# Attention loop unrolled with the softmax one head ahead, and a new order at the passage to the experts

## The chip, the cores and the metric

One core of one Trainium2 chip. The metric is the device time of one execution in microseconds (us), lower is better. The matrix engine (PE), the vector engine (DVE), the scalar engine (ACT), the small-step engine (POOL, GpSimd) and the queue that issues most weight transfers (SP, SyncE) each run a program of their own, and meet only at semaphores.

## What is computed

One layer over 256 prompt frames and 32 sample frames (288 rows, model width 2048), in float32:

```python
h = rms_norm(x, g_mix)
q_sb, k_sb, v_sb, q_sw, k_sw, v_sw, gate_pre = split(h @ w_in)    # 8 heads x 128; SWA has 2 kv heads
o_sb = stick_breaking(q_sb, k_sb, v_sb)        # exp(log_sigmoid(z) + sum of later log_sigmoid(-z))
o_sw = swa(rope(q_sw), rope(k_sw), v_sw, sink) # window of 2 chunks of 64, softmax with a sink
g = sigmoid(gate_pre + b_gate)
x = x + (g_sb * (o_sb @ w_sb_o) + g_swa * (o_sw @ w_swa_o)) @ w_out
x = x + hier_moe(rms_norm(x, g_ffn))           # best group of 4, then 2 of its 4 gated experts
y = rms_norm(x, g_final)
```

The sample frames attend to 128 cached frames besides their own. New keys and values are outputs as well, in float32.

## The kernel before

Float32 accuracy is reached by splitting each operand into a high and a low part and adding three products (L958, L959, L960 in `products`). A "block" is 128 output columns: 16 steps of 128 rows by three matmuls of 288 columns, 48 matmuls. For each block ACT makes the high part of the weights (`wh`, L635) and DVE the low part (`wl`, L1328, in `split`); SP fetches the weights into a ring, two blocks at a time.

The stages follow one another on PE:

- Projections: Q, K, V of the stick-breaking part, Q of the sliding window, then two K and two V blocks (KVSW). During the first, POOL zeroes the 4.5 MB of `y_rows` that overflowing experts would use: one memset and five DMAs of up to 1 MB.
- Sample attention: for each of the two kv groups, one after the other, scores (PE), maximum (DVE), exponent (ACT), divide (DVE, `zw`, L1426), transpose (PE, L1022), copy (ACT, L716), product with the values (PE, L1026).
- Attention: 8 heads in a loop over pairs. A head on PE is: scores `z`, a gate block, the suffix sums C (L1059), the transposes of the window's probabilities `zw` (L1066), a gate block, the two value products (L1073 and on). Softplus (ACT `lg`, DVE `spb`) and softmax (ACT L703, DVE L1426) of a head lie between its own `z` and its own C. ACT changes its table twice in a head (Exp to Ln and back).
- Second products: `o` of both attentions is split by ACT (`oh`, 16 copies of 288 columns) and DVE (`ol`, 16 subtractions); then 32 blocks, gates and products in turn, merged into `m` (parts `mh`, `ml`, L1478).
- Last projection: 16 blocks k. After block k PE runs, for block k-1, `turn_x` (transposes of the new residual times the norm weight, `xg`) and `logits` (router, needs `wr`, scaled by DVE in L1526). DVE adds the residual into `xT` (L1486); `xT` is fetched from HBM by a POOL DMA at the start of this stage. After each fourth block ACT and DVE cut the transposed residual into three bf16 parts (`parts_high` on ACT, `parts_rest` on DVE with `x2r`, L1495) for the exact gather.
- Passage and experts: routing on DVE, `choose` (L1613) makes the 0/1 matrix `pick` that gathers 64 slots for an expert on PE (L1157). 16 experts have 12 weight pieces of 1 MB each; a hand-written ORDER lists the 192 pieces, and at each piece t ACT makes its high part (L372), DVE its low part (L367, `slot_lo`), PE the products (L1176, L1179). `further_steps` and `row_numbers` (L1670 to L1721: slot weights, counts, the row numbers of the final gather) run on DVE at t = 2. `slot_rms` (PE) collects the norm of the slots.
- End: indirect gather of each token's two expert rows, weighted sum, final norm.

The lines at the last projection:

```python
for k in range(KT):
    pe.wait_ge(S["ev_d"], EV_OUT_D + k)
    products(IT_OUT + k // 4, k % 4, mh, ml)
    if k:
        turn_x(k - 1)
        pe.wait_ge(S["wr_scaled"], 1)
        logits(k - 1)
```

Of the kernel before, what the change touches and what calls it, by code (L numbers as in the profile page):

```python
# [173 lines left out]
def build(nc, x_prompt, x_sample, cache_sb_k, cache_sb_v, cache_swa_k, cache_swa_v, w_in, b_gate, swa_sink,  # L174
# [45 lines left out]
    st = at("st", 189.25, [P, 16])  # L220
    kcw_nat = at("kcw_nat", 189.5, [P, KV * HD])
    rope_a = at("rope_a", 181, [P, NT])
    rope_b = at("rope_b", 182.25, [P, NT])
    zero = at("zero", 184, [P, 512])
# [39 lines left out]
    stack_b = at("stack_b", 205.90625, [TAIL, DEC], BF16)  # L264
# [55 lines left out]
    with ExitStack() as ctx:  # L320
# [189 lines left out]
        def _(pool):  # L510
# [43 lines left out]
            for n in range(2):  # L554
                with pool.Fori(0, 2) as ii:
                    i = ii + 2 * n
                    for j in range(4):
# [4 lines left out]
                        else:  # L562
# [5 lines left out]
                              sb_kv_sample[ds(i, 1)].rearrange("a p n -> p (a n)"))  # L568
            pool.wait_ge(S["rope_done"], 11)

            for g in range(KV):
                pool.tensor_copy(qst[:, g * P:(g + 1) * P].rearrange("p (h n) -> p h n", h=GRP),
                                 qT[:, H + GRP * g:H + GRP * g + GRP, SEQ:NT]).then_inc(S["qst_st"], 1)
            pool.wait_ge(S["nat_done"], 21)
            pool.tensor_copy(v_sw[:], nat[:, :, KV * HD:]).then_inc(S["pool_head"], 1)
            nat_store(4, nat[:, 1, :], swa_kv_prompt, swa_kv_new)

            pool.wait_ge(S["pool_head"], 18)  # L580
            pool.wait_ge(S["vc_in"], 16)
            pool.wait_ge(S["kc_sb"], 2)
            with pool.Fori(0, IT_PROJ - IT_ATT) as i:
                for u in range(2):
                    hd = i * 2 + u
                    pool.wait_ge(S["z_sb"], hd + 1)
                    pool.tensor_copy(kst[:, 0:3, :], kT_sb[:, ds(hd, 1), :].rearrange("p a (t n) -> p (a t) n", n=P))\
                        .then_inc(S["kst_st"], 1)
                    pool.tensor_copy(kst[:, 3:4, :], kcT_sb[:, ds(hd, 1), :]).then_inc(S["kst_st"], 1)
                    pool.wait_ge(S["z_sw"], hd + KV)  # L590
                    pool.tensor_copy(qst[:].rearrange("p (a n) -> p a n", a=1),
                                     qT[:, ds(i + (H + GRP * u), 1), 0:SEQ]).then_inc(S["qst_st"], 1)
                    pool.wait_ge(S["o_sb"], hd + 1)
                    pool.tensor_copy(vst[:, 0:3, :], v_sb[:, :, ds(hd * P, P)]).then_inc(S["vst_st"], 1)
                    pool.tensor_copy(vst[:, 3:4, :], vc_sb[:, ds(hd * P, P)].rearrange("p (a n) -> p a n", a=1))\
                        .then_inc(S["vst_st"], 1)
# [22 lines left out]
        def _(act):  # L619
# [70 lines left out]
            act.wait_ge(S["pool_head"], 17)  # L690
            for j in range(4):
                step(IT_KVSW, j, None if j < 2 else lambda: a_.activation(
                    headT[:, j, 0:NT], main(j), ACT.Copy).then_inc(S["ev_a"], 1))
            act.wait_ge(S["kc_ps"], 3)
            a_.activation(kcT_sw[:], ps[6][:, 0:KV * P].rearrange("p (h n) -> p h n", h=KV), ACT.Copy)\
                .then_inc(S["kc_sb"], 1)

            def softmax(segments, sink, n):

                act.wait_ge(S["zw_done"], n)
                for c, (a, b) in enumerate(segments):
                    a_.activation(zw[:, a:b], zw[:, a:b], ACT.Exp, bias=st[:, 2 + c:3 + c],  # L703
                                  accum_out=st[:, 4 + c:5 + c]).then_inc(S["sums_done"], 1)
                c = len(segments)
                a_.activation(st[:, 6:6 + c], st[:, 2:2 + c], ACT.Exp, bias=sink).then_inc(S["sums_done"], 1)

            act.wait_ge(S["small_in"], 16 * 13)
            for g in range(KV):  # L710
                softmax([(0, SSC)], sinks_s[:, g:g + 1], g + 1)
                act.wait_ge(S["pT_ps"], g + 1)
                if g:
                    act.wait_ge(S["o_sw"], g)
                a_.activation(pT[:, 0:P], ps[5][:, 0:P], ACT.Copy).then_inc(S["pT_sb"], 1)
                a_.activation(pT[0:DEC, P:2 * P], ps[5][0:DEC, P:2 * P], ACT.Copy).then_inc(S["pT_sb"], 1)  # L716
                act.wait_ge(S["o_sw"], g + 1)
                a_.activation(qT[:, H + GRP * g:H + GRP * g + GRP, SEQ:NT],
                              ps[7][:, 0:P].rearrange("p (h n) -> p h n", h=GRP), ACT.Copy)\
                    .then_inc(S["o_sw_ev"], 1)  # L720
# [3 lines left out]
            with act.Fori(0, IT_PROJ - IT_ATT) as i:  # L724
                own.enter(i, 4)
                for u in range(2):
                    hd = i * 2 + u

                    act.wait_ge(S["zm_done"], hd + 2)
                    own(a_.activation(lg[:], zm[:], ACT.Abs))  # L730
                    own.wait()
                    own(a_.activation(lg[:], lg[:], ACT.Exp, scale=-1.0))
                    own.wait()
                    a_.activation(lg[:], lg[:], ACT.Ln, bias=1.0).then_inc(S["l_done"], 1)
                    softmax([(0, P), (P, SWC)], sinks[:, ds(i + GRP * u, 1)], hd + (KV + 1))

                    def gate(j):
                        return lambda: a_.activation(flat(gates[:, ds(i * 4 + j, 1), :]), main(j), ACT.Identity,
                                                     bias=par[:, ds(i * 4 + j, 1)]).then_inc(S["ev_a"], 1)
                    step(i + IT_ATT, 2 * u, gate(2 * u))  # L740
                    act.wait_ge(S["e_done"], hd + 2)
                    a_.activation(spb[:], lg[:], ACT.Exp).then_inc(S["a_done"], 1)
                    act.wait_ge(S["pT_ps"], hd + (KV + 1))
                    act.wait_ge(S["o_sw"], hd + KV)
# [10 lines left out]
            for h in range(2 * H):  # L755
                a_.activation(oh[:, h, :], qT[:, h, :], ACT.Copy).then_inc(S["oh_done"], 1)
# [4 lines left out]
            for r0 in (0, DEC, 2 * DEC):  # L761
                a_.activation(stack_b[r0:r0 + DEC, :], con[r0:r0 + DEC, r0:r0 + DEC], ACT.Copy)\
                    .then_inc(S["ident_done"], 1)
# [1058 lines left out]
```

## Time and profile before

| what | value |
|---|---|
| median of 3 runs | 1393.62 us (1389.62 to 1393.69) |
| profiled execution, its own time | 1389.65 us |
| its span | 1387.9 us |
| PE busy | 1237.8 us, 89% |
| DVE busy | 923.9 us, 67% |
| ACT busy | 790.1 us, 57% |
| mean granted PE clock | 0.968 of full speed |
| moved by DMA | 345.71 MB, 249 GB/s |

The span is what the profile covers; 1.7 us lie around it. A row in brackets such as [4.33 <-DVE wl L1328] says that the engine was idle for 4.33 us before this instruction, and that the end of DVE's instruction for `wl` of line 1328 let it go on. The granted clock is a share of 2.4 GHz: 1.00 is 2.4 GHz, 0.50 is 1.2 GHz.

### The profile page before, as it was taken

The numbers are of one execution on the slowest core, as the hardware profiler recorded it, in microseconds if no ns is written. First come the engines' busy times: TensorE is split into PE (matmuls) and PEld (weight loads), VectorE is DVE, ScalarE is ACT, GpSimd is POOL, SyncE is SP. The second block draws the span as 40 slices with busy tenths as digits, with TensorE's granted clock in tenths as the row PEclk, the third lists the DMA queues.
The fourth block names the chain that finished last, engine by engine and source line by source line (L and its number), as shares of the span: only waits on it lengthen the run. The fifth ranks groups of instructions, "written<-read, shape, count | busy, mean of one in ns | idle before, by whom it ended". The sixth has DMA issues, their size and how long they took to land.

```text
span 1387.9 us, 21824 instructions
## 1 busy us (share of the span) xinstructions
PE 1237.8 (89%) x8964; PEld 1079.3 (78%) x8964; DVE 923.9 (67%) x902; ACT 790.1 (57%) x761; POOL 63.9 (5%) x109
## 2 busy tenths in 40 slices
PE   5889999979999899999999957999999999999861
PEld 3789999969898899999899945666676666666650
DVE  3633345644444545454455585999999999999967
ACT  3423333235655744544444454888888888888852
POOL 2100010011221000000000000000000000000010
PEclk9999999989999999999999978999999999999995
DMA  8484545441322353553645756999999999999954
GB/s 262 154 302 152 186 146 190 169 145 61 121 96 86 123 171 130 181 181 128 243 146 187 296 199 224 363 410 413 414 414 414 416 416 414 414 413 413 416 186 171
DMA packets 187155, 345.71 MB, mean 249 GB/s; under 512 B 5328, under 2 KB 107840, under 8 KB 176080
## 3 DMA queue, kind: packets, MB, share of 16 engines
q1 hardware_dynamic: 182352, 322.72, 62.7%
q0 software_dynamic: 4336, 18.53, 3.8%
q10 hardware_dynamic: 400, 3.51, 0.6%
q8 instruction: 49, 0.80, 0.2%
q14 instruction: 18, 0.15, 0.0%
HBM read 321.86 MB, written 23.07 MB: 249 GB/s over the span
## 4 chain that ended last, share of the span: by engine, by line
PE 49%; DVE 34%; ACT 8%; issue 4%; DMA 4%; ACTq 0%; DVEq 0%; POOL 0%; POOLq 0%; SPq 0%
DVE slot_lo L367 24%; PE bank L958 14%; PE bank L960 13%; PE bank L959 13%; ACT eh L372 3%; PE bank L1176 3%; DVE y_sb L1653 2%; ACT wh L635 2%; DMA ring<-in_w_in 1%; DVE hgx L1632 1%; PE bank L1186 1%; PE bank L936 1%; DVE wl L1328 1%; DMA con<-in_const 1%; DMA yb<-y_rows,rows 1%
## 5 line engine op out<-in xcount | busy, mean ns | idle before, releaser
L367 DVE TENSOR_TENSOR slot_lo<-slot,eh 128x2048 fp32r<-128x2048 f32 x192 | 431.4, 2280 | 11.9 <-ACT eh L372 11.9
L372 ACT ACTIVATE eh<-slot 128x2048 fp32r<-128x2048 f32 x192 | 359.8, 1908 | 31.4 <-PE bank L1179 16.3
L1328 DVE TENSOR_TENSOR wl<-ring,wh 128x2048 fp32r<-128x2048 f32 x100 | 229.1, 2293 | 212.5 <-ACT wh L635 212.4
L958 PE MATMUL bank<-xh,wh 128*128 128x288 f32 x1088 | 331.6, 305 | 9.7 <-DVE xl L1336 5.1
L959 PE MATMUL bank<-xl,wh 128*128 128x288 f32 x1088 | 324.1, 298 | 0.0
L960 PE MATMUL bank<-xh,wl 128*128 128x288 f32 x1088 | 323.3, 297 | 0.0
L635 ACT ACTIVATE wh<-ring 128x2048 fp32r<-128x2048 f32 x100 | 190.8, 1909 | 131.0 <-PE bank L960 120.5
L958 PEld LDWEIGHTS bank<-xh,wh 128*128 128x128 f32 x1088 | 206.7, 190 | 14.5 <-issue 8.4
L959 PEld LDWEIGHTS bank<-xl,wh 128*128 128x128 f32 x1088 | 207.7, 191 | 0.3
L960 PEld LDWEIGHTS bank<-xh,wl 128*128 128x128 f32 x1088 | 207.9, 191 | 0.0
L1176 PE MATMUL bank<-slot_lo,hgx 128*128 128x512 f32 x512 | 146.1, 408 | 28.5 <-DVE slot_lo L367 26.6
L1176 PE MATMUL bank<-eh,hgx 128*128 128x512 f32 x512 | 150.8, 417 | 5.0 <-DVE hgx L1632 3.7
L1176 PEld LDWEIGHTS bank<-slot_lo,hgx 128*128 128x128 f32 x512 | 93.9, 191 | 67.8 <-DVE slot_lo L367 49.4
L1176 PEld LDWEIGHTS bank<-eh,hgx 128*128 128x128 f32 x512 | 90.1, 193 | 19.3 <-DVE hgx L1632 4.2
L1157 PEld LDWEIGHTS bank<-pick,x 128*128 128x128 bf16 x1536 | 60.3, 101 | 40.6 <-issue 32.7
L1179 PE MATMUL bank<-slot_lo,aTx 128*128 128x512 f32 x256 | 72.9, 406 | 10.5 <-DVE slot_lo L367 9.9
L958 PE MATMUL bank<-mh,wh 128*128 128x288 f32 x256 | 77.2, 302 | 2.7 <-DVE ml L1478 2.7
L958 PE MATMUL bank<-oh,wh 128*128 128x288 f32 x256 | 76.6, 299 | 3.3 <-DVE wl L1328 3.3
L1157 PE MATMUL bank<-pick,x 128*128 128x64 bf16 x1536 | 71.3, 197 | 7.2 <-DVE pick L1613 7.2
L959 PE MATMUL bank<-ol,wh 128*128 128x288 f32 x256 | 76.3, 298 | 0.0
L960 PE MATMUL bank<-oh,wl 128*128 128x288 f32 x256 | 75.9, 297 | 0.0
L959 PE MATMUL bank<-ml,wh 128*128 128x288 f32 x256 | 75.5, 295 | 0.0
(319 smaller groups left out, 1508.4 us busy)
## 6 DMA issues: line engine op xcount, KB each, us to landing
ring<-in_w_in SPq DMA_DIRECT2D x34, 2048.0 KB, 7.9
slot<-in_w_e_gate SPq DMA_DIRECT2D x64, 1024.0 KB, 10.2
slot<-in_w_e_up SPq DMA_DIRECT2D x64, 1024.0 KB, 9.8
slot<-in_w_e_down SPq DMA_DIRECT2D x64, 1024.0 KB, 10.7
ring<-in_w_out SPq DMA_DIRECT2D x8, 2048.0 KB, 8.0
ring<-in_w_sb_o SPq DMA_DIRECT2D x8, 1024.0 KB, 5.1
ring<-in_w_swa_o SPq DMA_DIRECT2D x8, 1024.0 KB, 7.4
y_rows<-y_sb SPq DMA_DIRECT2D x15, 512.0 KB, 10.0
```

The lines of the kernel that those rows point to most:

```text
L367: v.tensor_tensor(slot_lo[i][:], slot[i][:], eh[t % EH][:].bitcast(F32), ALU.subtract)\
L372: a_.activation(eh[t % EH][:], slot[t % CH][:], ACT.Copy).then_inc(S["hi_ready"], 1)
L635: a_.activation(wh[:, j % 2], raw(j), ACT.Copy).then_inc(S["wh_ready"], 1)
L936: mm = tr(ps[2 + k % 3][:, t * P:t * P + n], x_nat[0:n, t, k * P:(k + 1) * P], ident[0:n, 0:n])
L958: mm_(dst, wh[:, j % 2, k, :], hi[:, k, :], start=(k == k0), stop=False)
L959: mm_(dst, wh[:, j % 2, k, :], lo[:, k, :], start=False, stop=False)
L960: mm = mm_(dst, wl[:, j % 2, k, :], hi[:, k, :], start=False, stop=(k == k1 - 1))
L1157: mm_(out, x2[j][:, t, k * P:(k + 1) * P], p_[:, t, 0:SLOTS], start=(t == 0 and j == 0), stop=False)
L1176: mm = mm_(ps[2 + j // 4], hgx[:, kt, :], part[:, c * 512:(c + 1) * 512], start=(low == 0 and kt == 0), stop=(low == 1 and kt == KT - 1))
L1179: mm = mm_(ps[bank0 + c], aTx[par_][:, j - 8, :], part[:, c * 512:(c + 1) * 512], start=(low == 0 and j == 8), stop=(low == 1 and j == CH ...
L1328: v.tensor_tensor(wl[:, j % 2], raw(j), wh[:, j % 2].bitcast(F32), ALU.subtract)\
L1653: v.tensor_tensor(y, y, banks[0:SLOTS, y_banks(s, h)], ALU.add).then_inc(S["y_dve"], 1)
```

## The change

1. The zeroing of `y_rows` moves from before the first store of POOL to behind the K block's store; its tile `zero` gets another address, which the sample's `pTg` shares later.
2. The attention is unrolled. Both kv groups of the sample go through one softmax (`zg`, `pTg`), whose scores follow KVSW block 2, together with the scores of head 0; the cache's transposes follow block 0. From there `z`, softplus and softmax of head hd+1 are made during head hd: PE's `head_z(hd + 1)` stands behind the transposes of head hd.
3. `oh` and `ol` are made in 4 + 4 instructions of 1152 columns instead of 16 + 16. The four `both` copies go behind the loop of the second products, three `stack_b` copies go away.
4. Last projection: block 0 may start before the last two `ml`, `turn_x` and `logits` of block k-1 run inside block k ahead of its step 8, and the sum of squares inside block 15 ahead of its step 13.
5. Passage: the high parts of the first expert pieces stand ahead of the last bf16 parts and of `tokens_high`; the first low parts ahead of `rparts`; `slot_rms` moves behind piece 2; `further_steps` and `row_numbers` move from t = 2 to t = `WHEN[0, 7] + 2` = 9; seven small steps of slot weights (`weights`) and ACT's two exponents for them go to the very end.

Cut to its core, in the order of the file (tiles, POOL, ACT, PE, DVE):

```diff
+    zg = at("zg", 190.5, [P, 2 * SSC])
+    pTg = at("pTg", 201, [P, 4 * P])
...
-            pool.memset(zero[:], 0.0).then_inc(S["zero_set"], 1)
-            pool.wait_ge(S["zero_set"], 1)
-            for r0, k in ((NE * SLOTS, 4), (NE * SLOTS + 4 * P, 0)):
-                n, m = (P, k) if k else (MAXOV * SLOTS - 4 * P, 1)
-                for q in range(m):
-                    pool.dma_start(y_rows[r0 + q * P:r0 + q * P + n, :].rearrange("p (b n) -> p b n", n=512),
-                                   zero[0:n, :].rearrange("p (a n) -> p a n", a=1).to_broadcast([n, 4, 512]))\
-                        .then_inc(S["zero_out"], 16)
...
+                if n == 0:
+                    pool.memset(zero[:], 0.0).then_inc(S["zero_set"], 1)
+                    pool.wait_ge(S["zero_set"], 1)
+                    for r0, k in ((NE * SLOTS, 4), (NE * SLOTS + 4 * P, 0)):
+                        n, m = (P, k) if k else (MAXOV * SLOTS - 4 * P, 1)
+                        for q in range(m):
+                            pool.dma_start(y_rows[r0 + q * P:r0 + q * P + n, :].rearrange("p (b n) -> p b n", n=512),
+                                           zero[0:n, :].rearrange("p (a n) -> p a n", a=1).to_broadcast([n, 4, 512]))\
+                                .then_inc(S["zero_out"], 16)
...
+            def softplus(hd):
+
+                act.wait_ge(S["zm_done"], hd + 2)
+                if hd:
...
+                own(a_.activation(lg[:], lg[:], ACT.Exp, scale=-1.0))
...
+            for hd in range(H):
...
+                step(it, 2 * u, gate(2 * hd))
+                if hd == 0:
+                    act.wait_ge(S["pT_ps"], 1)
+                    act.wait_ge(S["zero_out"], 16 * 5)
+                    a_.activation(pTg[:, 0:2 * P], ps[5][:, 0:2 * P], ACT.Copy).then_inc(S["pT_sb"], 1)
...
+                act.wait_ge(S["e_done"], hd + 2)
+                a_.activation(spb[:], lg[:], ACT.Exp).then_inc(S["a_done"], 1)
+                act.wait_ge(S["pT_ps"], hd + 2)
+                if hd:
+                    act.wait_ge(S["o_sw"], hd + 1)
+                a_.activation(pT[:], ps[5][:, 0:SWC], ACT.Copy).then_inc(S["pT_sb"], 1)
+                if hd + 1 < H:
+                    softplus(hd + 1)
+                    softmax(hd + 1)
+                    log_part(hd + 1)
+                step(it, 2 * u + 1, gate(2 * hd + 1))
+                if hd == 0:
+                    act.wait_ge(S["o_sw"], 1)
...
+                act.wait_ge(S["o_sb"], hd + 2)
+                a_.activation(qT[:, hd, :], ps[6][:, 0:NT], ACT.Copy).then_inc(S["o_sb_ev"], 1)
...
+            for h in range(0, 2 * H, 4):
+                a_.activation(oh[:, h:h + 4, :], qT[:, h:h + 4, :], ACT.Copy).then_inc(S["oh_done"], 1)
...
+            parts_copy(4)
             act.wait_ge(S["blk"], upto(IT_END - 1, 3))
+            high(0)
+            parts_mid(4)
+            high(1)
+            tokens_high(0)
...
-            for t in range(EH):
-                high(t)
-            tokens_high(0)
-            slot_rstd(0)
...
+                if t == EH:
+                    slot_rstd(0)
...
+            act.wait_ge(S["ex_in"], 2)
+            a_.activation(gex, gex, ACT.Exp).then_inc(S["ex_out"], 1)
+            a_.activation(d21, d21, ACT.Exp).then_inc(S["ex_out"], 1)
...
+                        if k in mid:
+                            mid[k]()
...
+                        if parted and k >= KT - 2:
+                            pe.wait_ge(S["ml_done"], k + 2)
...
+                if j == 2:
...
+                    head_z(0)
...
+            gate_block(0)
...
+            pe.wait_ge(S["p_ready"], 1)
...
+            for hd in range(H):
+                pe.wait_ge(S["sp_done"], hd + 1)
+                pe.wait_ge(S["e_done"], hd + 1)
...
+                pe.wait_ge(S["p_ready"], hd + 2)
+                pe.wait_ge(S["pT_sb"], hd + 2)
+                for c in range(3):
+                    mm = tr(ps[5][:, c * P:(c + 1) * P], zw[:, c * P:(c + 1) * P], ident)
+                mm.then_inc(S["pT_ps"], 1)
+                if hd + 1 < H:
+                    head_z(hd + 1)
+                gate_block(2 * hd + 1)
...
+                head_o(hd)
+                if hd + 1 < H:
+                    gate_block(2 * hd + 2)
...
-            pe.wait_ge(S["ml_done"], KT + 1)
+            pe.wait_ge(S["ml_done"], KT - 1)
...
-                products(IT_OUT + k // 4, k % 4, mh, ml)
-                if k:
...
+                def behind():
                     turn_x(k - 1)
                     pe.wait_ge(S["wr_scaled"], 1)
                     logits(k - 1)
+
+                def squares():
+                    pe.wait_ge(S["ev_d"], EV_OUT_D + KT)
+                    pe.wait_ge(S["sq_sum"], KT - 1)
+                    pe.wait_ge(S["x2_r"], 3 * 4)
+                    ssq(sqacc, True)
+
+                mid = {8: behind, 13: squares} if k == KT - 1 else {8: behind} if k else {}
+                products(IT_OUT + k // 4, k % 4, mh, ml, parted=(k == 0), mid=mid)
...
-            pe.wait_ge(S["rp_done"], 1)
-            slot_rms(pick[0])
...
+                if t == 2:
+                    pe.wait_ge(S["rp_done"], 1)
+                    slot_rms(pick[0])
...
+            for hd in range(H):
...
+                split((2 * u + 2) % 4, b0 + 3)
+                dve.wait_ge(S["c_done"], hd + 1)
+                v.tensor_tensor(lg[:], zm[:], ps[3][:, 0:SBC], ALU.subtract).then_inc(S["e_done"], 1)
+                if hd + 1 < H:
+                    scores(hd + 1)
+                split((2 * u + 3) % 4, b0 + 4)
+                if hd + 1 < H:
+                    divide(zw, sth, 3 * hd + 10, heads)
+                dve.wait_ge(S["o_sw"], hd + 2)
+                v.tensor_copy(qT[:, H + GRP * u + hd // 2, 0:SEQ], ps[7][:, 0:SEQ]).then_inc(S["o_sw_ev"], 1)
+                if hd + 1 < H:
+                    softplus(hd + 1)
...
+            low(0)
+            tokens_low(0)
+            low(1)
...
-            low(0)
-            tokens_low(0)
...
+            def weights():
...
+            def further_steps():
...
-                if t:
+                if t > 1:
...
-                if t == EH - 1:
-                    further_steps()
-                    row_numbers()
...
+                if t == WHEN[0, 7] + 2:
+                    further_steps()
+                    row_numbers()
...
+            weights()
```

## Rows read from the trace of the kernel before

**Rows 1.** The page's chain that ended last, shares of the span by line.

```profile
DVE slot_lo L367 24%; PE bank L958 14%; PE bank L960 13%; PE bank L959 13%; ACT eh L372 3%; PE bank L1176 3%; DVE y_sb L1653 2%; ACT wh L635 2%; DMA ring<-in_w_in 1%; DVE hgx L1632 1%; PE bank L1186 1%; PE bank L936 1%; DVE wl L1328 1%; DMA con<-in_const 1%; DMA yb<-y_rows,rows 1%
```

**Rows 2.** Windows: stretch, us, busy PE, PEld, DVE, ACT, POOL, granted clock, DMA share, GB/s.

```profile
321.50:464.30 142.80, 133.64 (x963) 128.46 (x962) 64.32 (x100) 81.81 (x123) 22.05 (x32) 1.00 0.30 103
464.30:678.00 213.70, 208.85 (x1550) 208.02 (x1548) 106.87 (x112) 106.76 (x121) 0.00 (x0) 0.99 0.47 157
678.00:800.00 122.00, 120.90 (x857) 110.12 (x857) 63.19 (x80) 54.54 (x73) 2.69 (x5) 1.00 0.62 218
...
868.00:1340.00 472.00, 437.63 (x3208) 322.09 (x3207) 467.33 (x267) 398.13 (x285) 0.00 (x0) 1.00 1.01 400
```

**Rows 3.** The chain in order of time: start us, us, what.

```profile
65.56 20.70 DMA ring<-in_w_in
...
1351.93 12.00 DMA yb<-y_rows,rows
```

**Rows 4.** Timeline of PE, first projection: start us, us, what, [idle before <-releaser].

```profile
90.66 0.37 PE L958 MATMUL bank<-xh,wh 128*128 128x288 f32 x1 [4.33 <-DVE wl L1328]
...
92.17 0.44 PE L959 MATMUL bank<-xl,wh 128*128 128x288 f32 x1
92.41 0.44 PE L960 MATMUL bank<-xh,wl 128*128 128x288 f32 x1
```

**Rows 5.** Queues of the DMA view, 75 to 85 us: packets, MB, share of 16 engines.

```profile
q0 software_dynamic: 822, 3.13, 76.2%
```

**Rows 6.** The page's DMA issues: us from issue to landing.

```profile
ring<-in_w_in SPq DMA_DIRECT2D x34, 2048.0 KB, 7.9
```

**Rows 7.** Timeline of SyncE's queue, 161 to 170 us.

```profile
163.86 0.37 SPq L414 DMA_DIRECT2D ring<-in_w_in  x1
```

**Rows 8.** Waits of PE, 260 to 520 us: us in total, times, longest.

```profile
PE bank L1066 <- DVE zw L1426: 9.2, 7, 1.4
PE bank L1022 <- DVE zw L1426: 7.6, 2, 5.1
```

**Rows 9.** Timeline of DVE, end of the K and V block stage.

```profile
288.98 2.29 DVE L1328 TENSOR_TENSOR wl<-ring,wh 128x2048 fp32r<-128x2048 f32 x1 [1.36 <-ACT wh L635]
```

**Rows 10.** Timeline of PE, first product C of the attention loop.

```profile
321.54 0.91 PE L1059 MATMUL bank<-spb,con 128*128 128x448 f32 x2
```

**Rows 11.** Timeline of ACT, third head of the attention.

```profile
355.72 1.28 ACT L734 ACT_TABLE_LOAD   x1
357.01 0.58 ACT L734 ACTIVATE lg<-lg 128x448 f32<-128x448 f32 x1
```

**Rows 12.** Timeline of ACT, then of PE, start of the second product stage.

```profile
469.70 5.46 ACT L756 ACTIVATE oh<-qT 128x288 fp32r<-128x288 f32 x16 [2.47 <-DVE qT L1456]
475.06 0.81 ACT L759 ACTIVATE con<-con 64x64 f32<-64x64 f32 x4
...
482.24 0.40 PE L958 MATMUL bank<-oh,wh 128*128 128x288 f32 x1 [3.25 <-DVE wl L1328]
```

**Rows 13.** Timeline of PE, then of DVE, last projection.

```profile
679.10 0.37 PE L958 MATMUL bank<-mh,wh 128*128 128x288 f32 x1 [2.70 <-DVE ml L1478]
...
714.50 0.49 PE L1106 MATMUL bank<-con,xg 128*128 128x128 f32 x3
...
688.43 0.45 DVE L1486 TENSOR_TENSOR xT<-xT,bank 128x288 f32<-128x288 f32 x1 [5.92 <-DMA xT<-xT_spill]
...
691.01 0.48 DVE L1526 TENSOR_TENSOR wr<-wr,par 128x320 f32<-128x320 f32 x1
...
719.22 1.28 DVE L1495 TENSOR_TENSOR x2r<-bank,x 128x512 f32<-128x512 f32 x2
```

**Rows 14.** Timeline of DVE, passage to the experts.

```profile
821.53 0.16 DVE L1674 TENSOR_REDUCE rt<-rt 128x3 f32<-128x12 f32 x1
...
828.41 0.17 DVE L1721 CAST rows<-rt 128x6 uint32<-128x6 f32 x1
...
868.49 8.90 DVE L367 TENSOR_TENSOR slot_lo<-slot,eh 128x2048 fp32r<-128x2048 f32 x4 [1.38 <-ACT eh L372]
```

More of the change, by code:

```diff
@@ L574, in _ @@
+            head_q(0)
             pool.wait_ge(S["nat_done"], 21)
             pool.tensor_copy(v_sw[:], nat[:, :, KV * HD:]).then_inc(S["pool_head"], 1)
+            head_v(0)
             nat_store(4, nat[:, 1, :], swa_kv_prompt, swa_kv_new)
             pool.wait_ge(S["pool_head"], 18)
[L581 to L596, printed above, removed]
@@ L598, in _ @@
+            for hd in range(1, H):
+                head_k(hd)
+                head_q(hd)
+                head_v(hd)
             pool.wait_ge(S["ml_done"], KT + 1)
@@ L709, in _ @@
[L709 to L720, printed above, removed]
+                if j == 0:
+                    act.wait_ge(S["kc_ps"], 3)
+                    a_.activation(kcT_sw[:], ps[6][:, 0:KV * P].rearrange("p (h n) -> p h n", h=KV), ACT.Copy)\
+                        .then_inc(S["kc_sb"], 1)
@@ L722, in _ @@
+                if j == 2:
+                    act.wait_ge(S["small_in"], 16 * 13)
+                    sample_softmax()
+                    softplus(0)
+                    softmax(0)
+                    log_part(0)
             act.wait_ge(S["nat_free"], 6)
             act.wait_ge(S["pool_head"], 18)
[L724 to L744, printed above, removed]
-                    a_.activation(pT[:], ps[5][:, 0:SWC], ACT.Copy).then_inc(S["pT_sb"], 1)
-                    step(i + IT_ATT, 2 * u + 1, gate(2 * u + 1))
-                    act.wait_ge(S["o_sb"], hd + 2)
-                    a_.activation(flat(qT[:, ds(hd, 1), :]), ps[6][:, 0:NT], ACT.Copy).then_inc(S["o_sb_ev"], 1)
-                own.leave(IT_PROJ - IT_ATT)
@@ L752, in _ @@
+            act.wait_ge(S["o_sw"], 1 + H)
             act.wait_ge(S["vst_st"], 2 * H)
             act.wait_ge(S["o_sb_ev"], H + 1)
[L754 to L760 removed]
@@ new lines, in divide, with softplus @@
+            def divide(z, st_, sums, segments):
+                dve.wait_ge(S["sums_done"], sums)
+                then(v.tensor_tensor(st_[:, 8:10], st_[:, 4:6], st_[:, 6:8], ALU.add))
+                then(v.reciprocal(st_[:, 10:12], st_[:, 8:10]))
+                for n, (a, b) in enumerate(segments):
+                    ins = v.tensor_scalar(z[:, a:b], z[:, a:b], st_[:, 10 + n:11 + n], None, ALU.mult)
+                ins.then_inc(S["p_ready"], 1)
+            def softplus(hd):
+                dve.wait_ge(S["l_done"], hd + 1)
+                dve.wait_ge(S["o_sb"], hd + 1)
+                v.scalar_tensor_tensor(out=spb[:], in0=zm[:], scalar=0.0, in1=lg[:], op0=ALU.max, op1=ALU.add)\
+                    .then_inc(S["sp_done"], 1)
@@ L1390, in _ @@
+            heads = [(0, P), (P, SWC)]
             for j in range(4):
@@ L1459, in _ @@
-            for h in range(2 * H):
-                dve.wait_ge(S["oh_done"], h + 1)
-                v.tensor_tensor(ol[:, h, :], qT[:, h, :], oh[:, h, :].bitcast(F32), ALU.subtract)\
+                if j == 2:
+                    dve.wait_ge(S["small_in"], 16 * 13)
+                    sample_scores()
+                    scores(0)
+                    divide(zg, st, 4, [(0, SSC), (SSC, 2 * SSC)])
+            divide(zw, sth, 7, heads)
+            softplus(0)
+            for hd in range(H):
+                u = hd % 2
+                b0 = 4 * (IT_ATT + hd // 2) + 2 * u
+                split((2 * u + 2) % 4, b0 + 3)
[10 more added lines that the diff above has]
+                    softplus(hd + 1)
```

308 lines of the change are left out of this document (157 added, 151 removed).

## The prediction

> **What bounds the kernel now.** I read the page's chain first. It runs through PE's three products of a step (L958 to L960, 40% of the span together) up to the last projection, and through DVE's low part of the expert weights (L367, 24%) from there [rows 1]. The reader should see two regimes. The windows by stage say how tight each is: in the attention PE is busy for 133.64 of 142.80 us, in the second products for 208.85 of 213.70, in the last projection for 120.90 of 122.00, all at a granted clock of 0.99 or 1.00; in the experts DVE is busy for 467.33 of 472.00 us [rows 2]. So until about 800 us a step is worth what PE stands idle or runs at the lower clock, and in the experts only what starts DVE's train earlier; nothing within it. I then read the chain in order of time, for transfers in it: one load of the weight ring (20.70 us) and the final gather (12.00 us) are the two that matter here [rows 3]. The timelines of PE, DVE and ACT around each edit gave the rest.
>
> A block is 48 matmuls; 32 blocks in 208.85 busy us [rows 2] make 6.5 us a block, 0.136 us a matmul.
>
> **1. Zero stores, -5.8 us.** PE stands still for 4.33 us in the first projection and then issues every 0.24 us (92.17 to 92.41) in place of 0.136 [rows 4], which is the 1.2 GHz level, for some 14 matmuls: 14 x 0.104 = 1.5. Cause: the ring load before it took 20.70 us [rows 3] against a median of 7.9 [rows 6], and while it was under way the zero stores moved 3.13 MB in 10 us, 76.2% of the DMA engines' time [rows 5]. By that rule, the trace agrees: 822 packets of the zero stores carried 3.13 MB [rows 5], and the fight could come again wherever both are under way (rival a). At the new place the stores follow the K store. A ring load is issued at 163.86 [rows 7], and the stores come some 4 to 5 us later by the spacing of POOL's steps before; over half the load is then through, and a rest of about 1 MB at the rate the load got before (about 0.1 MB a us, 2.1 MB in 20.70 us) ends near 179, where ACT wants it near 180 by the run of blocks. I take 0 as the new cost, with 5.8 as the other bound: before, the load was issued together with the stores and had no lead. ACT's copies of the sample's probabilities now wait for the zero stores (same address), with the rest of ACT's attention queued behind; the stores have over 100 us until then, so 0. On POOL the V store and the copies for head 0 are queued behind five DMA issues; POOL is busy 22.05 of 142.80 us there [rows 2], so 0 too.
>
> **2. From KVSW to the first C, -12.6 us.** The serial sample softmax holds PE for 7.6 us at two waits [rows 8], and more in short ones. The last `wl` that matters is done at 288.98 + 2.29 = 291.27 [rows 9], the first C comes at 321.54 [rows 10]. Afterwards: sample scores 1.5 us on DVE, then on ACT exponents, softplus and softmax of head 0 with two table changes of 1.28 us each [rows 11], together 8 us; ACT then evacuates the last KVSW block near 300, PE has stood for about 4 us, and one gate block (6.5, plus 1.6 if it begins at the low clock) and the transposes follow: C near 308.95. 321.54 - 308.95 = 12.6. Bounds 10 (0.1 for each of some 25 small steps that I cost from neighbours) and 14 (a table load ahead of the wait).
>
> **3. Heads, -6 us.** The seven waits for `zw` hold 9.2 us [rows 8]; counted from start to start they cost 1.45 each, 10 in all. They go, as softmax(hd+1) has two gate blocks to run in. What is late next is the chain by ACT and DVE from one gate block to the next C: evacuation, high part, low part, subtraction, Exp, copy, softplus, softmax, Ln, gate evacuation, high part, low part, divide, copy and `spb` add up to 18.1 us with one table load inside, against a PE period of 17.75 (two blocks and 4.6 of small products): at most 0.35 a head, 2.5 in all. The first head pays 1.5 for its extra copies. 10 - 2.5 - 1.5 = 6. The Trainium skill, "ScalarE: Activation LUTs", section "What ACT_TABLE_LOAD costs", puts a switch at 1.28 us plus a drain of 1.38. The trace shows no drain: the load starts at 355.72 and the next ACTIVATE at 357.01 [rows 11], and I go by the row; by that rule the chain would be 21 us a head and the gain gone (rival c).
>
> **4. Start of the second products, -4.0 us.** 16 copies take 5.46 us and the `both` copies 0.81 ahead of the first high part [rows 12]. Four copies of 1152 columns take about 4 x 1.05 = 4.2 on ACT, but PE needs the first group and ACT's queue is shorter by 1.26 + 0.81 + 0.73 (the three dropped ones), so PE's wait of 3.25 [rows 12] falls to 0.8 (gain 2.5), and the low clock that follows it (1.5, as in step 1) does not come. Bounds 2.5 and 4.8. The `both` copies go where ACT has 1.9 of 6.5 us to do.
>
> **5. Last projection, +12.1 us.** The wait of 2.70 for `ml` [rows 13] goes: -2.7 at most, since block 0 may start two steps early. But the work for block k-1 now sits in the middle of block k, and PE runs in order: what it waits for there, it waits for with the block's second half behind it. Three places:
> - Block 1 needs the residual of block 0, which waits for `xT` from HBM until 688.43, and `wr` scaled at 691.01 + 0.48 [rows 13]; PE would be at step 8 near 687. Before, that wait was hidden by a whole block. Net of the 2.7 I get the start of block 2 2.3 later, or 3.9 with 1.6 at the low clock behind so long a hole; I take 3.9, as the 4.33-us hole [rows 4] had it.
> - Blocks 5, 9 and 13 begin the next group of x2, whose banks come free when DVE has made `x2r`, behind its `wl`: 719.22 + 1.28 for the first two tiles [rows 13]. PE's step 8 comes 3.2 us after the block's start (714.50 + 1.1 of old order [rows 13]), DVE ends 5.4 to 6.0 after it. 2.5 us each, 7.5 together; 1.5 more each if the clock falls.
> - The residual of block 15 is no longer covered by the logits of block 14: 0.7.
>
> Sum 3.9 + 7.5 + 0.7 = 12.1; bounds 10.5 and 17. At all other blocks the work ahead is in time, by some 0.3 us, so the edit costs nothing there; `xg` of the block before is what comes last.
>
> **6. Passage, -3.7 us.** DVE's train of 2.29-us low parts has gaps until 868.49 [rows 14], and none that matter after [rows 2]. `further_steps` and `row_numbers` lie in it at 821.53 to 828.41 [rows 14], 7 us with the weights, 6.0 without. They go from piece 2 to piece 9, still ahead of the start of the train, so moving them gives nothing by itself; `low(0)` and `low(1)` ahead of the small steps, and `slot_rms` out of PE's way, give 3.7 (bounds 0 and 6). The weights cost about 1 us at the end, and their two exponents as little, under the 12.00 us of the final gather [rows 3]: nothing. Without that cover they would cost 2.
>
> **Sum.** -5.8 - 12.6 - 6.0 - 4.0 + 12.1 - 3.7 = -20.0. On the profiled execution's own 1389.65: 1369.65, that is **1370**. The median of the runs is 4 us above that execution, so a median of the new kernel may lie at 1374.
>
> **Rivals.**
> (a) The zero stores meet the ring load at the new place as they did at the old: +5.8, 1375.5. For it: 3.13 MB in 10 us [rows 5]; against: the load has a lead of 4 us. It decides if the load is not down by 180.
> (b) The waits inside the last projection are covered (DVE puts `x2r` first, or `xT` lands earlier because POOL is ahead): -8.2, 1361.5. Against: the queue order on DVE is the code's.
> (c) The table loads drain: the heads' gain of 6 turns to a loss of 2.6, 1378.3. Against: the two starts 1.29 apart [rows 11].
> (d) The experts are paced by the weight stream (DMA share 1.01, 400 GB/s [rows 2]), so that an earlier start of DVE is waited off: 3.7 lost, 1373.4. Against: ACT, which waits for the pieces, shows no DMA among its releasers there.
> (e) Slower: each stall inside a block puts PE's clock at the low level for the blocks after it. A block at 1.2 GHz costs 48 x 0.104 = 5.0 more; all 14 would give +70, 1440. It decides from some four blocks, 20 us. For it: [rows 4] show the low level after a 4.33-us hole; against: the clock reads 1.00 in the last projection after the 2.70-us hole [rows 2, 13].
>
> **How the numbers follow.** Chances: as summed 0.50, (a) 0.13, (b) 0.14, (c) 0.05, (d) 0.11, (e) 0.07. A measurement of this kernel tells 0.3%, 4 us, from no change; (a) to (d) all stay on the faster side, and only several bounds at once (0.05, out of the 0.50) reach no change. Faster 0.88, same 0.05, slower 0.07. The likeliest one's own range by its bounds is 1362 to 1380; with (b) and (c) 1358 to 1382, which leaves out (e) and the ends of the others, under 2 in 10.
>
> **What would show it.** Right: the ring load issued near 65 lands in 8 us and the hole at 86 to 91 is gone; the first C near 303 (321.5 less 5.8 and 12.6); no wait for `zw` in the heads, and short ones for `spb`; the second products start with a hole under 1 us; PE waits inside blocks 1, 5, 9 and 13 for `wr`, `xg` and `x2r`; DVE's train begins 19 to 25 us earlier than 868.49. Wrong: a hole after 176; a clock under 0.9 in the last projection; heads over 18.3 us apart.

## The result and the profile after

The changed kernel takes 1380.11 us (median of 5 runs, 1379.08 to 1382.35) against 1393.52 us before (1388.89 to 1393.69): ratio 0.9927, 95% interval 0.9914 to 0.994. By the ratio it is faster by 0.7%, about 10 us, half of what was forecast; the two medians lie 13.4 us apart. The time is just inside the range's upper end of 1382. The profiled executions, whose rows are used below, have spans of 1387.9 and 1379.0 us, 8.9 apart.

The windows by stage of the changed kernel, in the columns of [rows 2]. They are cut at the same marks, moved: first C, first value product of head 7, start of the last projection, its end, start of DVE's train. (At the third mark the window before ends 1.1 us ahead of the first product with `mh`.)

```profile
303.60:445.60 142.00, 136.46 (x971) 131.15 (x969) 64.39 (x100) 83.48 (x127) 14.37 (x35) 0.98 0.34 117
445.60:653.40 207.80, 207.28 (x1550) 206.57 (x1548) 104.92 (x97) 104.38 (x101) 0.00 (x0) 1.00 0.48 162
653.40:795.00 141.60, 129.67 (x860) 116.53 (x858) 64.48 (x83) 54.48 (x77) 2.70 (x5) 0.94 0.52 186
795.00:860.00 65.00, 42.89 (x430) 33.83 (x429) 47.03 (x114) 31.96 (x31) 0.00 (x0) 0.79 0.63 232
860.00:1330.00 470.00, 436.63 (x3194) 321.43 (x3191) 465.81 (x266) 396.84 (x283) 0.00 (x0) 1.00 1.01 401
```

The reader should see that the second products lost their hole (207.80 us against 213.70), that the attention's 142.00 us are as long as before, and that the last projection, 122.00 us before, now has 12 us of idle PE and a clock of 0.94.

Marks read from the two timelines give the sum term by term:

| mark | before | after | shift | gained since the mark before |
|---|---|---|---|---|
| first C | 321.54 | 303.67 | -17.87 | -17.87 (forecast -18.4, steps 1 and 2) |
| first value product of head 7 | 464.29 | 445.64 | -18.65 | -0.78 (forecast -6, step 3) |
| first product with `oh` | 482.24 | 460.86 | -21.38 | -2.73 (step 4, its hole) |
| first product with `mh` | 679.10 | 653.43 | -25.67 | -4.29: 1.5 from step 4's low clock, 2.8 from the early block 0 of step 5 |
| copy of the logits | 799.44 | 794.39 | -5.05 | +20.62 (step 5; with the 2.8, +17.8; forecast +12.1) |
| start of DVE's train | 868.49 | 860.00 | -8.49 | -3.44 (forecast -3.7, step 6) |
| end of the span | 1387.9 | 1379.0 | -8.9 | -0.4 |

Two terms are off: the heads by 5.2 us, the last projection by 5.7. The rest is within a microsecond, though not always for the reason forecast (step 6 below).

**The heads.** PE's timeline around the first C of the changed kernel, then that of ACT and of POOL:

```profile
303.67 0.92 PE L1116 MATMUL bank<-spb,con 128*128 128x448 f32 x2
...
310.42 0.87 PE L1123 MATMUL bank<-con,zw 128*128 128x128 f32 x3 [5.46 <-ACT pTg L768]
...
322.70 0.70 PE L1088 MATMUL bank<-spb,vst 128*128 128x256 f32 x2
...
331.18 0.91 PE L1116 MATMUL bank<-spb,con 128*128 128x448 f32 x2
...
340.80 0.59 PE L1088 MATMUL bank<-spb,vst 128*128 128x256 f32 x2
```

```profile
307.46 0.50 ACT L741 ACTIVATE gates<-bank,par 128x288 f32<-128x288 f32 x1 [10.48 <-POOLq L544]
...
309.65 0.37 ACT L767 ACTIVATE pTg<-bank 128x256 f32<-128x256 f32 x1
```

```profile
296.79 0.83 POOL L604 COPY v_sw<-nat 128x768 f32<-128x768 f32 x1 [13.04 <-DVE nat L1413]
297.56 2.57 POOL L594 COPY vst<-v_sb 128x384 f32<-128x384 f32 x1
...
300.32 0.58 POOL L541 DMA_DIRECT2D out<-nat  x1
300.89 0.51 POOL L542 DMA_DIRECT2D out<-nat  x1
307.60 0.51 POOL L580 COPY kst<-kT_sb 128x384 f32<-128x384 f32 x1 [6.20 <-DMA out<-nat]
```

Read from PE back. Its wait of 5.46 us names ACT's copy `pTg`. ACT had been free since 297, and its first gate eviction waited 10.48 us for POOL's queue, line 544: that is `nat_free`, raised when the output stores of the last K and V block have landed. ACT waits for it ahead of all gates, because gates and the stored tile `nat` share memory. Before, that wait lay under the sample's serial softmax; now the first gate is due 18 us earlier and the stores come behind POOL's copies for head 0, one of which took 2.57 us beside DVE's low part. The prediction costed ACT's new waits, but not this old one, whose cover the change takes away.

The later place of the stores also makes them slower. This is their time from issue to landing, the changed kernel first, then the kernel before:

```profile
out<-nat POOLq DMA_DIRECT2D x1, 256.0 KB, 6.2
out<-nat POOLq DMA_DIRECT2D x1, 64.0 KB, 6.5
```

```profile
out<-nat POOLq DMA_DIRECT2D x1, 256.0 KB, 2.3
out<-nat POOLq DMA_DIRECT2D x1, 64.0 KB, 2.1
```

In the changed kernel a ring load of 2 MB is issued at 299.93, just ahead of the stores at 300.32 and 300.89, and the DMA engines are 87% busy until they land. In the kernel before, the stores go out at 295.89 and 296.46 and that load only at 298.26.

PE pays more than the 5.46 us: its clock is at 0.50 from 309 to 315. From the first C to the first value product it takes 322.70 - 303.67 = 19.03 us, and 9.62 (331.18 to 340.80) in the next head, as in all later ones. So the first head costs 9.4 us, where the prediction had 1.5.

**The last projection.** Waits of PE from 640 to 795 us, changed kernel (us in total, times, longest):

```profile
PE bank L1160 <- DVE x2r L1570: 6.8, 6, 2.0
PE bank L1160 <- ACT xg L839: 3.8, 1, 3.8
PE bank L1168 <- DVE wr L1601: 0.8, 1, 0.8
PE bank L1168 <- DVE xT L1561: 0.5, 1, 0.5
```

And PE's timeline in blocks 1 and 5:

```profile
667.05 0.90 PE L1160 MATMUL bank<-con,xg 128*128 128x128 f32 x3 [3.80 <-ACT xg L839]
668.76 1.15 PE L1168 MATMUL bank<-xT,wr 128*20 128x288 f32 x2 [0.80 <-DVE wr L1601]
...
702.72 0.33 PE L1160 MATMUL bank<-con,xg 128*128 128x128 f32 x1 [1.99 <-DVE x2r L1570]
703.31 0.28 PE L1160 MATMUL bank<-con,xg 128*32 128x128 f32 x1 [0.27 <-DVE x2r L1570]
...
704.76 0.44 PE L1002 MATMUL bank<-mh,wl 128*128 128x288 f32 x1
705.00 0.44 PE L1000 MATMUL bank<-mh,wh 128*128 128x288 f32 x1
```

The waits are where the prediction put them and as long: 3.8 + 0.8 in block 1, 2.26 in each of blocks 5, 9 and 13 (a third of 6.8). Behind each, the matmuls come every 0.24 us (704.76 to 705.00), the lower level of the clock, in blocks 5, 9 and 13 too, where the prediction took it to stay up. Two windows of 2 us show it for blocks 9 and 13 (granted clock 0.57 and 0.54):

```profile
738.00:740.00 2.00, 2.00 (x9) 1.66 (x8) 1.94 (x5) 0.77 (x2) 0.00 (x0) 0.57 0.00 0
774.00:776.00 2.00, 2.00 (x11) 2.00 (x10) 0.60 (x1) 0.00 (x0) 0.00 (x0) 0.54 0.49 189
```

### The profile page after: what moved, and what is told of

It is laid out like the page before. It is cut to its first block, busy times and chain, and to the rows that moved or that the text cites. A ratio compares the mean times of both kernels' runs of the same rounds, so it can differ in the third digit from the quotient of the medians.

```text
span 1379.0 us, 21485 instructions
## 1 busy us (share of the span) xinstructions
PE 1238.0 (90%) x8964; PEld 1080.1 (78%) x8964; DVE 923.1 (67%) x886; ACT 788.4 (57%) x744; POOL 59.2 (4%) x109
## 4 chain that ended last, share of the span: by engine, by line
PE 54%; DVE 34%; ACT 5%; DMA 3%; issue 3%; POOL 0%; ACTq 0%; POOLq 0%; DVEq 0%
DVE slot_lo L369 24%; PE bank L1000 15%; PE bank L1002 14%; PE bank L1001 14%; ACT eh L374 3%; DVE y_sb L1728 2%; PE bank L1234 2%; DVE hgx L1707 1%; ACT wh L650 1%; PE bank L974 1%; DMA con<-in_const 1%; PE bank L1244 1%; DMA yb<-y_rows,rows 1%; DVE wl L1387 1%; DVE a L1716 1%
## 5 line engine op out<-in xcount | busy, mean ns | idle before, releaser
L1000 PE MATMUL bank<-mh,wh 128*128 128x288 f32 x256 | 80.5, 314 | 0.0
L1002 PE MATMUL bank<-mh,wl 128*128 128x288 f32 x256 | 77.7, 304 | 0.0
```

Of the source, the lines that this page charges most:

```text
L1000: mm_(dst, wh[:, j % 2, k, :], hi[:, k, :], start=(k == k0), stop=False)
L1002: mm = mm_(dst, wl[:, j % 2, k, :], hi[:, k, :], start=False, stop=(k == k1 - 1))
```

## The experiments

Each is the changed kernel with one edit, timed beside the kernel before; the changed kernel's own 1380.11 is the base, and a gain is a difference of medians. The kernel before had medians of 1389.69 to 1391.45 in these runs, so a difference of medians and one of ratios can be 1 us apart; both are given where more is.

**nat_first.**

```diff
+            pool.dma_start(swa_kv_prompt, nat[:, 1, :]).then_inc(S["nat_out"], 16)
+            pool.dma_start(swa_kv_new, nat[0:DEC, 2, :]).then_inc(S["nat_out"], 16)
             pool.tensor_copy(v_sw[:], nat[:, :, KV * HD:]).then_inc(S["pool_head"], 1)
             head_v(0)
-            nat_store(4, nat[:, 1, :], swa_kv_prompt, swa_kv_new)
+            pool.wait_ge(S["nat_out"], 4 * 32 + 32)
+            pool.sem_inc(S["nat_free"], 1)
```

> The changed kernel with one edit: POOL issues the two output stores of the last K and V block before its copies for head 0, and waits for their landing after them. Theory A (the attention's missing 5 us are ACT's first gate eviction, held until these stores have landed, because the wait for them stands ahead of all gates): the wait of PE for pTg of 5.46 us falls to about 2, the low clock behind it goes, -5 to -6 us, 1374 to 1375. Theory B (the ACT and DVE chain of a head is longer than PE's two blocks, so any slack is eaten in the next heads): the first head gets shorter, the others longer by as much, 1379 to 1380.

Measured: 1374.29 us, ratio to before 0.9888 (0.9867 to 0.9908), 5.8 less than the changed kernel. Theory A holds. PE's wait for `pTg` (us in total, times, longest) falls from 5.46 us to:

```profile
PE bank L1126 <- ACT pTg L771: 1.5, 1, 1.5
```

The clock is 1.00 in each 2-us window from 303 to 311. The stores go out at 296.05, ahead of the ring load at 298.50, and land in 2.3 and 2.2 us. ACT's first gate eviction no longer waits for POOL but for the end of PE's block:

```profile
302.58 0.50 ACT L744 ACTIVATE gates<-bank,par 128x288 f32<-128x288 f32 x1 [6.58 <-PE bank L1005]
```

The edit moves the stores both ahead of POOL's copies and out of the load's way; what each is worth by itself was not tried.

**act_wait_late.**

```diff
-            act.wait_ge(S["nat_free"], 6)
-            act.wait_ge(S["pool_head"], 18)
             for hd in range(H):
...
+                if hd == 1:
+                    act.wait_ge(S["nat_free"], 6)
+                    act.wait_ge(S["pool_head"], 18)
                 step(it, 2 * u + 1, gate(2 * hd + 1))
```

> The changed kernel with one edit: ACT waits for the stores and for the copy of v_sw only ahead of gate block 3, since blocks 0 to 4 do not lie on the stored tile. POOL's order stays. Theory A: the wait for pTg falls to about 1.3 us, but POOL's copies of head 1's keys still stand behind the landing, so PE waits about 1 us for them right after; -4 to -5 us, 1375 to 1376. If it is POOL's queue and not ACT's wait that holds the head, PE's wait only moves from the transposes to the scores of head 1 and less than 2 us are gained.

Measured: 1378.61 us, ratio 0.9917 (0.9898 to 0.9937), 1.5 less than the changed kernel: under 2, which is what was expected if POOL's queue holds the head. PE's timeline and the windows behind it:

```profile
306.01 0.52 PE L1124 MATMUL bank<-con,zw 128*128 128x128 f32 x3 [1.45 <-ACT pTg L766]
308.32 1.22 PE L1041 MATMUL bank<-qT,kst 128*128 128x256 f32 x2 [1.80 <-POOL kst L582]
```

```profile
309.00:311.00 2.00, 2.00 (x10) 1.91 (x9) 0.30 (x1) 0.19 (x1) 0.00 (x0) 0.50 0.00 0
311.00:313.00 2.00, 2.00 (x9) 1.82 (x8) 1.15 (x4) 1.16 (x2) 0.00 (x0) 0.50 0.00 0
313.00:315.00 2.00, 2.00 (x10) 2.00 (x9) 0.57 (x3) 1.28 (x6) 0.00 (x0) 0.50 0.00 0
```

ACT's wait is gone, but POOL still stands in its own wait for the landing, with head 1's keys behind it (`kst`). Two waits of 1.45 and 1.80 us in place of one of 5.46, and then the low clock for 6 us and more. So the wait was passed on: the stores hold ACT and POOL alike, and of the two edits only issuing them first frees both.

**out_after.**

```diff
-                mid = {8: behind, 13: squares} if k == KT - 1 else {8: behind} if k else {}
-                products(IT_OUT + k // 4, k % 4, mh, ml, parted=(k == 0), mid=mid)
+                products(IT_OUT + k // 4, k % 4, mh, ml, parted=(k == 0))
+                if k:
+                    behind()
+                if k == KT - 1:
+                    squares()
```

> The changed kernel with the transposes and logits of block k-1 behind block k again, and the squares behind block 15; block 0 still starts two ml early. Theory A (waits inside blocks 1, 5, 9 and 13, and the low clock behind them, cost 8.3 and three times 4.2 us; a start of block 0 that is 2.7 us early is paid back at the wait for xT): -17 to -18.5 us, 1362 to 1363, and PE waits for wr or xg once, behind block 1, 2 us or so. Rival (the clock is low in this stage whatever the order): -10 to -12, 1369.

Measured: 1363.28 us, ratio 0.9803 (0.9784 to 0.9822), 16.8 less than the changed kernel. All of PE's waits up to the end of the stage:

```profile
PE bank L1168 <- DVE wr L1604: 1.2, 1, 1.2
PE bank L1160 <- ACT xg L839: 1.0, 1, 1.0
```

**out_some** puts the work behind the block in blocks 1, 5, 9 and 13 alone:

```diff
+                late = k in (1, 5, 9, 13)
+                mid = {8: behind, 13: squares} if k == KT - 1 else {8: behind} if k and not late else {}
...
+                if late:
+                    behind()
```

> The changed kernel with the work for block k-1 inside block k, except in blocks 1, 5, 9 and 13, where it stands behind the block. Theory A: all the waits lie in these four blocks, so the time is that of the kernel with all of it behind, within 1 us (1362 to 1363). Rival (the work in the middle of a block costs something at every block, by breaking PE's stream): longer than that by 12 times 0.3 us or more.

Measured: 1364.8 us, ratio 0.9811 (0.979 to 0.9831): 1.5 more than out_after, intervals overlapping. Nearly all of the loss is in the four blocks.

**out_mid14** (`{14: behind}` for `{8: behind}`; block 15 keeps its `{8: behind, 13: squares}`).

> The changed kernel with the work for block k-1 ahead of step 14 of block k instead of step 8 (block 15 as it was). PE comes to it 2.4 us later. Theory A (the loss is a wait with a fixed end plus the low clock it brings): the waits for x2r of 2.3 us each fall under 0.5 and the clock stays up, that for xg in block 1 falls to 1.4; -14 to -16 us, 1364 to 1366. Rival (the place inside a block costs, whatever the wait): under 8 us gained.

Measured: 1364.72 us, ratio 0.9809 (0.9782 to 0.9836), 15.4 less than the changed kernel. PE's waits in the stage:

```profile
PE bank L1160 <- ACT xg L839: 1.2, 1, 1.2
PE bank L1168 <- DVE wr L1601: 1.2, 1, 1.2
```

The six waits for `x2r` have gone. Being inside a block costs little by itself (1.4 us over out_after, within the intervals); being there before the data costs the rest. From the first product with `mh` to the copy of the logits it takes 126.12 us here and 124.32 in out_after.

**out_old** is out_after with `ml_done` waited for in full ahead of block 0 (`KT + 1`, no `parted`).

> The changed kernel with the last projection wholly in the old order: work for block k-1 behind block k, and block 0 waiting for all ml. Theory A (the early start of block 0 is worth nothing, because the wait for xT behind block 1 takes it back): the same time as with the early start, 1363 within 1 us; PE waits 2.7 us for ml and no longer for xg or wr. Rival (the early start is worth its 2.7 us): 1366.

Measured: 1363.57 us, ratio 0.9808 (0.9791 to 0.9824), the same as out_after. Between these two the early start is worth nothing: PE's only wait there is the old one, and those of 1.2 and 1.0 us for `wr` and `xg` are gone.

```profile
PE bank L1000 <- DVE ml L1556: 2.7, 1, 2.7
```

Both have a low clock behind their wait. Here it is the same wait of 2.70 us that left the clock at 1.00 in the kernel before:

```profile
656.00:658.00 2.00, 2.00 (x10) 2.00 (x9) 2.00 (x1) 0.40 (x3) 0.00 (x0) 0.50 0.87 267
```

**zero_back** puts the zeroing back ahead of the first store (its tile at the old address, ACT's wait ahead of the sample's softmax).

> The changed kernel with the zeroing of the overflow rows at its old place ahead of the first store, its tile at the old address and ACT's wait for it ahead of the sample's softmax. Theory A (the ring load is starved by the zero stores there and not at the new place): PE's hole near 86 us and the low clock behind it come back, +5.8 to +6.1, 1386. Rival (the hole has another cause, such as the load's own place): no change.

Measured: 1385.67 us, ratio 0.996 (0.9949 to 0.9972), 5.6 more than the changed kernel. PE's hole and the ring load in the chain come back:

```profile
90.61 0.37 PE L1001 MATMUL bank<-xh,wh 128*128 128x288 f32 x1 [4.00 <-DVE wl L1388]
```

```profile
65.83 20.37 DMA ring<-in_w_in
```

**further_early** puts `further_steps` and `row_numbers` back at piece 2.

> The changed kernel with further_steps and row_numbers back at piece 2, as before the change. Theory A (the passage's gain of about 3.4 us is from the order of the first low parts, tokens and slot_rms; 6.0 us of small steps stand ahead of choose for expert 2 in either place): within 1 us of 1380. Rival (the gain is from moving these steps): +3 us or more, 1383.

Measured: 1383.62 us, ratio 0.9948 (0.9931 to 0.9965), 3.5 more. The rival was right. From the copy of the logits to the start of the train it takes 861.90 - 792.62 = 69.28 us in this kernel, 69.05 before and 65.61 in the changed one: all of the passage's gain is from moving these steps. DVE's timeline of this kernel, then of the changed one, says why:

```profile
822.09 0.17 DVE L1799 CAST rows<-rt 128x6 uint32<-128x6 f32 x1
...
847.92 2.29 DVE L369 TENSOR_TENSOR slot_lo<-slot,eh 128x2048 fp32r<-128x2048 f32 x1 [3.48 <-ACT eh L374]
850.13 0.55 DVE L1688 TENSOR_TENSOR pick<-con,rk 128x384 bf16<-128x384 f32 x1
```

```profile
843.36 0.17 DVE L1799 CAST rows<-rt 128x6 uint32<-128x6 f32 x1
843.44 4.49 DVE L369 TENSOR_TENSOR slot_lo<-slot,eh 128x2048 fp32r<-128x2048 f32 x2
847.84 0.55 DVE L1688 TENSOR_TENSOR pick<-con,rk 128x384 bf16<-128x384 f32 x1
```

Ahead of the last low part before `choose` (847.92), DVE stands for 3.48 us waiting for ACT. At piece 9 the small steps fill that time, and the low parts follow them without a wait (843.44); at piece 2 they add to the way there.

**further_late** puts them right behind `choose` for expert 2.

> The changed kernel with further_steps and row_numbers right behind choose for expert 2, where DVE then waits 9.8 us for ACT and PE in the profile. Theory A: these 6.0 us come out of PE's wait of 7.3 us for pick, and the train of low parts starts 5 to 6 us earlier: 1374 to 1375. Rival (the train waits for weights or for ACT there): under 2 us gained.

Measured: 1378.59 us, ratio 0.9901 (0.9875 to 0.9927), 1.5 less than the changed kernel by the medians and 3.6 by the ratios, with intervals that overlap. From the logits on, `choose` for expert 2 comes 2.0 us earlier than in the changed kernel and the train 2.3, not 5 to 6: the 3.58-us wait for ACT ahead of the last low part is back, so only what exceeds it is won. The small steps are now hidden, as DVE's timeline shows:

```profile
852.72 0.17 DVE L1799 CAST rows<-rt 128x6 uint32<-128x6 f32 x1
...
856.38 0.43 DVE L1721 TENSOR_TENSOR aTx<-bank,aTx 128x256 fp32r<-128x256 f32 x1 [3.49 <-ACT aTx L887]
```

**best_f** takes nat_first, act_wait_late, out_after and further_late together; **best_m** has out_mid14 in place of out_after.

> The changed kernel with the stores issued first on POOL, ACT's wait for them ahead of gate block 3, the work for block k-1 behind block k, and further_steps behind choose for expert 2. If the gains lie in different stretches and add: 1380.1 less 5.8, 16.8 and 2.3 makes 1355; ACT's later wait adds up to 0.7. Rival (an earlier passage meets the weight stream, which is then the bound of the experts): 1358 to 1360.

> As the combination before, but with the work for block k-1 ahead of step 14 of block k in place of behind it. If the place inside the block is free once nothing waits: 1355 to 1357, no more than 1.5 from the other. Rival (it pays at the end, where block 15's residual is hidden): 1353 to 1354.

Measured: best_f 1353.03 us, ratio 0.973 (0.9713 to 0.9747); best_m 1357.1 us, ratio 0.976 (0.9744 to 0.9777). best_f is 27.1 us faster than the changed kernel, where the single gains sum to 5.8 + 16.8 + 1.5 = 24.1, so they add and 3 us more, and 37 us faster than the kernel before. Some 2 us of the surplus lie in the last projection: from the first product with `mh` to the copy of the logits it takes 122.16 us, and 124.32 in out_after. The experts don't meet a limit of the weight stream: 25.0 us of lead over the changed kernel at the logits are 28.2 at the end.

best_m is 4 us longer, where 1.5 was allowed, and all of that lies in the same stretch, 126.30 us. Its waits in block 1 are 1.4 and 1.2 us and best_f's 0.4 and 1.2; behind them the clock falls in best_m and not in best_f, as these windows show, two of best_m and then best_f's:

```profile
664.00:666.00 2.00, 2.00 (x11) 2.00 (x10) 0.45 (x1) 0.95 (x1) 0.00 (x0) 0.53 0.04 13
666.00:668.00 2.00, 2.00 (x11) 2.00 (x11) 1.01 (x1) 1.73 (x3) 0.00 (x0) 0.62 0.00 0
```

```profile
662.00:664.00 2.00, 1.68 (x10) 1.21 (x11) 2.00 (x3) 1.24 (x3) 0.00 (x0) 1.00 0.77 274
```

Two windows at 0.53 and 0.62 lose about 1.7 us and the longer wait 1.0; the remaining 1.4 or so is not accounted for. In best_f the early start of block 0 is worth little too: the stretch takes 122.16 us against 121.86 + 2.70 of wait in out_old, and of these 2.4 some 1.7 are out_old's low clock (0.82, 0.50 and 0.82 in the three windows from 654 to 660).

## Why the prediction was wrong, point by point

- **Step 1, zero stores: right.** The load issued at 66.87 no longer stands in the chain, the hole is gone, and zero_back brings back 5.6 us (forecast 5.8). The stores behind the K store took 9 to 16 us each to land and held nobody. They did meet a ring load, as rival (a) had it: its lead was 2.3 us (issued at 159.09, the stores from 161.34) and not 4 to 5, and it took 11.8 us against a median of 7.9. But no engine waited for it: the slack, more than the lead, kept the cost at 0.
- **Step 2, from KVSW to the first C: right.** -17.87 for steps 1 and 2 together against -18.4.
- **Step 3, heads: failed, +5.2 us.** The waits for `zw` are gone and the head's period is 17.76 us (low parts at 351.48 and 369.24), so the chain of 18.1 that was to cost 2.5 did not bind. The failing step is "The first head pays 1.5 for its extra copies", with the sentence on POOL in step 1, "POOL is busy 22.05 of 142.80 us there [rows 2], so 0 too": the first head cost 9.4, and the 2.5 that did not come due hides a part of the miss. The sentence on POOL prices what stands in front of a wait by how busy POOL is. POOL is idle most of the time, but it is waiting in order, for a transfer. nat_first, which moves only that transfer's issue, gains 5.8 us. So the period was forecast well, and the first head was not followed through to its old waits. (ACT's wait for the zero stores, which step 1 put at 0 as well, did cost nothing.)
- **Step 4, second products: right.** The hole fell from 3.25 to 0.52 us (forecast 0.8) and the low clock behind it went: -2.73 and -1.5, against -4.0.
- **Step 5, last projection: the mechanism right, the size not.** Each of blocks 5, 9 and 13 cost 4.2 us where 2.5 was summed; block 1 8.4 gross where 6.6 was (DVE's low parts behind block 1 are at 694.12 before and 676.87 after, 17.25 earlier, from 25.67; behind block 5 at 724.16 and 711.09, 13.07 earlier). The difference is the lower clock, which the text had as an upper bound (1.5 more each) and did not take; rival (e) had against it that a hole of 2.70 us left the clock up. The 0.7 for block 15 did not show. The sum of 17.8 lies past the bound of 17. Rival (b), covered waits, is out; of rival (e) a piece came true, in the blocks with a wait and not through the stage (0.94 over it).
- **Step 6, passage: the size right, the cause wrong.** "Moving them gives nothing by itself" failed: further_early shows that moving is all of the 3.4 us. It was argued from their place ahead of the train; what decides is DVE's wait for ACT inside that stretch, which takes them up. The new order of the first low parts and of `slot_rms`, to which the 3.7 was put down, gives nothing (69.28 us against 69.05), so the hit on 3.7 is luck. The weights at the end cost nothing: DVE does them by 1335.5 us and then waits for the gather until 1349.23.
- **Rival (c)** is out: the period stayed at PE's 17.76 us with two table changes in each head. Its price was also too low by its own figures: 21 us a head against 19.3 before would lose some 12 us, not 2.6. **Rival (d)** is out: best_f carries its whole lead through the experts. **Rival (a)** is in step 1.

What the table rests on is one execution each; the mark of the first C lay between 301.4 and 304.4 us in the runs that leave the start alone, so single marks are good to some 1.5 us.

## What to carry to other kernels

When a change pulls a stage forward, look at every wait that the first instruction of that stage has, the old ones above all: a wait that was never seen in the profile because other work covered it is the next one to show. A step moved into the stream of the engine that bounds the kernel must be late enough for its data, not early enough for its result: six steps later gave back 15 us here. And a block of small steps belongs where its engine already waits.

## What the runs showed of the hardware

- The clock did not fall with the length of one hole alone. A single wait of 2.70 us ahead of block 0, in the kernel before, left it at 1.00 [rows 2, 13], and one of 1.53 in nat_first did too; the same wait of 2.70 in out_old was followed by 0.50. Waits of 1.99 and 0.27 us among small matmuls in block 5 were followed by a spacing of 0.24 us, and waits of 1.45 and 1.80 in act_wait_late by 0.50 for three windows of 2 us. In block 1, waits of 1.35 and 1.16 in best_m were followed by 0.53 and 0.62, and 0.39 and 1.15 in best_f by 1.00. Six us at half the clock lose 3 us, which in act_wait_late is about as much as the waits. What tells these cases apart was not tried.
- A POOL copy of 128x384 took 2.57 us at 297.56, beside DVE's low part of 297.01 to 299.76 (2.75 us in place of 2.29), and 0.51 us at 306.03 for the same copy in the kernel before, where DVE had only small steps to do: both were slower beside each other. The Trainium skill, "GPSIMD Engine Reference", section "Specifications", says that GpSimd shares its SBUF interfaces with VectorE and that the two contend when a VectorE instruction has two SBUF inputs; the low part is such an instruction (ring and `wh`), so the trace agrees. No run here changed it by itself.
- The same two stores of 256 and 64 KB took 2.3 and 2.1 us to land before, and 6.2 and 6.5 in the changed kernel, where a 2 MB ring load had been issued 0.4 us ahead of them. In nat_first, issued 2.5 us ahead of that load, they took 2.3 and 2.2. It is the fight of step 1 the other way round: there the stores held up the load.
